# State space mixer of two transformer blocks: another layout of the Toeplitz rows, a later load of the residual, filler products on TensorE, and another order of the last products

## The reference, cut to what matters

```python
lam_bar = jnp.exp(lam * dt)
b_bar = ((lam_bar - 1.0) / lam)[..., None] * b
bu = jnp.einsum('blgc,gpc->blgp', uf.astype(jnp.complex64), b_bar)
_, states = lax.associative_scan(_ssm_binop, (a_elems, bu), axis=1)
y = jnp.real(jnp.einsum('blgp,gcp->blgc', states, c))
y = y + d_skip.astype(f32).reshape(N_GROUPS, SSM_GROUP) * uf
z = jax.nn.gelu(y.reshape(bsz, length, D_MODEL)).astype(u.dtype)
zw = z @ w_glu
val, gate = zw[..., :D_MODEL], zw[..., D_MODEL:]
return val * jax.nn.sigmoid(gate)
```

## Time and profile before

| what | us |
|---|---|
| median of 3 runs | 2467.12 |
| lowest and highest | 2464.04, 2469.94 |
| the profiled execution's own time | 2473.14 |
| its span in the profile | 2471.4 |
| of it, up to the first product of the linear unit | 173.45 |

### The profile page before, as it was taken

One profiled execution on the slowest core, in us unless ns is written; L12 is line 12 of the kernel. 1 busy time (PEld: TensorE's weight loads), 2 busy tenths in 40 slices (PEclk: granted clock), 3 DMA queues, 4 the chain that ended last, 5 costly groups with the idle time before them and its releaser, 6 DMA issues.

```text
span 2471.4 us, 30025 instructions
## 1 busy us (share of the span) xinstructions
PE 2340.3 (95%) x10838; PEld 1938.3 (78%) x10838; DVE 1405.0 (57%) x1986; ACT 880.9 (36%) x1316; POOL 203.2 (8%) x154
## 2 busy tenths in 40 slices
PE   2779999999899999999999999999999899999999
PEld 2677788888788877888877778878888688888887
DVE  6855554456666665454447657773445547654443
ACT  3213332223445533222245435553434443322221
POOL 5502200002100030000020000002000001200000
PEclk7959999999999999999999989999999999999999
DMA  2352232222211112222222211213223212232222
GB/s 114 50 131 84 94 102 94 95 100 94 71 55 58 61 60 94 95 101 94 97 82 78 85 60 54 67 61 109 94 102 128 68 60 94 96 101 94 98 98 85
DMA packets 77174, 213.72 MB, mean 86 GB/s; under 512 B 18320, under 2 KB 26768, under 8 KB 76688
## 3 DMA queue, kind: packets, MB, share of 16 engines
q1 hardware_dynamic: 70880, 205.14, 25.6%
q10 hardware_dynamic: 6192, 7.19, 0.9%
HBM read 203.78 MB, written 4.19 MB: 84 GB/s over the span
## 4 chain that ended last, share of the span: by engine, by line
PE 83%; DVE 6%; ACT 4%; POOL 2%; DMA 2%; issue 2%; SPq 1%; ACTq 0%; DVEq 0%; POOLq 0%
PE lin L423 25%; PE lin L424 25%; PE lin L425 25%; ACT w_hi L811 1%; DVE w_lo L1179 1%; SPq L337 1%; PE tr L690 1%; POOL ssm_cl L1772 1%; PE tr L584 1%; POOL tmp_c L1771 1%; POOL ssm_cl L1770 1%; DMA cols<-cols 1%; DMA ssm_mt<-ssm_kp 1%; DVE fox_pl L1471 1%; PE tr L736 0%
## 5 line engine op out<-in xcount | busy, mean ns | idle before, releaser
L811 ACT ACTIVATE w_hi<-w_raw 128x1024 fp32r<-128x1024 f32 x369 | 390.8, 1059 | 1067.2 <-PE lin L425 1063.7
L423 PE MATMUL lin<-x_hi,w_hi 128*128 128x512 f32 x1472 | 594.8, 404 | 4.4 <-DVE w_lo L1179 2.6
L424 PE MATMUL lin<-x_lo,w_hi 128*128 128x512 f32 x1472 | 575.7, 391 | 0.0
L425 PE MATMUL lin<-x_hi,w_lo 128*128 128x512 f32 x1472 | 575.7, 391 | 0.0
L1179 DVE TENSOR_TENSOR w_lo<-w_raw,w_hi 128x1024 fp32r<-128x1024 f32 x369 | 468.7, 1270 | 110.3 <-ACT w_hi L811 109.6
L423 PEld LDWEIGHTS lin<-x_hi,w_hi 128*128 128x128 f32 x1472 | 278.5, 189 | 72.2 <-issue 9.5
L424 PEld LDWEIGHTS lin<-x_lo,w_hi 128*128 128x128 f32 x1472 | 278.4, 189 | 65.5 <-issue 9.5
L425 PEld LDWEIGHTS lin<-x_hi,w_lo 128*128 128x128 f32 x1472 | 277.8, 189 | 58.8
L423 PE MATMUL lin<-q_hi,w_hi 128*128 128x512 f32 x688 | 271.5, 395 | 7.9 <-DVE q_lo L1184 6.0
L424 PE MATMUL lin<-q_lo,w_hi 128*128 128x512 f32 x688 | 270.7, 394 | 0.0
L425 PE MATMUL lin<-q_hi,w_lo 128*128 128x512 f32 x688 | 270.4, 393 | 0.0
(11 more groups left out here) (405 smaller groups left out, 2858.3 us busy)
## 6 DMA issues: line engine op xcount, KB each, us to landing
w_raw<-w SPq DMA_DIRECT2D x369, 512.0 KB, 3.3
ssm_mt<-ssm_kp SPq DMA_DIRECT2D x64, 64.0 KB, 2.8
ssm_u<-x_a SPq DMA_DIRECT2D x1, 2048.0 KB, 12.2
resid<-x_b ACTq DMA_DIRECT2D x1, 2048.0 KB, 10.6
z_b<-z_scratch SPq DMA_DIRECT2D x4, 512.0 KB, 4.6
out<-resid SPq DMA_DIRECT2D x8, 256.0 KB, 2.1
z_scratch<-ssm_y SPq DMA_DIRECT2D x16, 64.0 KB, 2.3
z_scratch<-ssm_y ACTq DMA_DIRECT2D x16, 64.0 KB, 2.6
```

What stands on the lines that cost most here:

```text
L423: nc.tensor.matmul(out, WH[:, b, w], xh[:, k, 0:cols], start=(k == 0), stop=False)
L424: nc.tensor.matmul(out, WH[:, b, w], xl[:, k, 0:cols], start=False, stop=False)
L425: last = nc.tensor.matmul(out, WL[:, b, w], xh[:, k, 0:cols], start=False, stop=(k == KC - 1))
L811: nc.scalar.activation(WH[:, b, :], raw[:, r, :], ACT.Copy).then_inc(s_hi, 1)
```

## The change

There are four parts.

1. **Layout.** `KP` and `MT` hold the group as the innermost index instead of the second. A Toeplitz DMA then reads and writes one run of 4 KB per partition instead of 8 runs of 512 bytes. In return TensorE reads a within matrix with a step of 8 elements (32 bytes) between columns, ScalarE's copy into `KP` reads PSUM with a step of 128 elements and writes runs of 4, and GpSimd's addition has a step of 8.
2. **Residual.** ScalarE waits for all Toeplitz DMAs before it issues the load of `R`.
3. **Fillers.** `keep_clock(bank, n)` runs n float32 products of the identity with 512 columns of `U` into a bank that nobody needs then: 4 before kernels 2, 5 once VectorE has the block states (a new semaphore `s_mid`), 1 before within 7, and 6 in the first slab of the linear unit.
4. **Order.** within 6 stands between outflow 1 and outflow 2, within 7 between outflow 4 and outflow 5.

```diff
-    MT = at("ssm_mt", 40 * KB, [2, GB, P])
-    KP = ss("ssm_kp", 2 * GB * (2 * CH - 1) * GC * 4, [2, GB, 2 * CH - 1, GC])
+    MT = at("ssm_mt", 40 * KB, [2, CH, GC, GB])
+    KP = ss("ssm_kp", 2 * GB * (2 * CH - 1) * GC * 4, [2, 2 * CH - 1, GC, GB])
...
-            eng.dma_start(MT[j * GC:(j + 1) * GC, b % 2, :, :],
-                          KP[0:GC, b % 2, :, j:j + CH, :].rearrange("p g j c -> p g (j c)")).then_inc(s_mt[b % 2], 16)
+            eng.dma_start(MT[j * GC:(j + 1) * GC, b % 2, :, :, :], KP[0:GC, b % 2, j:j + CH, :, :]).then_inc(s_mt[b % 2], 16)
...
                 for k in range(KC):
                     if ready is not None:
                         pe.wait_ge(s_x, ready(k))
-                    if k == 3 and mid is not None:
+                    if k == mid_at and mid is not None:
                         mid()
...
-                    last = nc.tensor.matmul(WB[b][:, g * NK:(g + 1) * NK], MT[:, b % 2, g, :], U[:, b * GB + g, :],
+                    last = nc.tensor.matmul(WB[b][:, g * NK:(g + 1) * NK], MT[:, b % 2, :, :, g].rearrange("p j c -> p (j c)"), U[:, b * GB + g, :],
...
+            def keep_clock(bank, n):
+
+                for _ in range(n):
+                    nc.tensor.matmul(bank[:], ident[:], U[:, 0:GB, :].rearrange("p g k -> p (g k)"), start=True, stop=True)
...
+            pe.wait_ge(s_vr, BATCHES)
+            keep_clock(WB[5], 4)
+            for b in range(BATCHES - 2):
+                kernels(b + 2)
+                within(b)
+            pe.wait_ge(s_kp, 2 * BATCHES)
+            pe.wait_ge(s_mid, 1)
+            keep_clock(WB[7], 5)
+            for b in range(2):
+                outflow(b)
+            within(6)
+            for b in range(2, 5):
+                outflow(b)
+            keep_clock(WB[7], 1)
+            within(7)
+            for b in range(5, BATCHES):
+                outflow(b)
+
+            def glu_wait():
+
+                pe.wait_ge(s_z, 2)
+                keep_clock(LIN[1], 6)
+            stage("glu", QH, QL, ready=chunks(), mid=glu_wait, mid_at=6)
...
-                    nc.scalar.activation(KP[0:GC, b % 2, 4 * j:4 * j + 4, CH - 1:, :].rearrange("p g j c -> p g (j c)"),
-                                         SC[j][0:GC, :].rearrange("p (g n) -> p g n", g=4), ACT.Copy).then_inc(s_kp, 1)
+                    nc.scalar.activation(KP[0:GC, b % 2, CH - 1:, :, 4 * j:4 * j + 4],
+                                         SC[j][0:GC, :].rearrange("p (g j c) -> p j c g", g=4, j=CH), ACT.Copy).then_inc(s_kp, 1)
...
             act.wait_ge(s_kd, BATCHES)
+            for i in range(2):
+                act.wait_ge(s_mt[i], 16 * CH * BATCHES // 2)
             act.dma_start(R[:], a["x_b"]).then_inc(s_in[1], 16)
...
+            dve.sem_inc(s_mid, 1)
```

More of the change, by code:

```diff
@@ L321, in two_blocks @@
         s_pow, s_xt, s_kd = (sem(n) for n in ("powers_ready", "power_tables", "kp_d_added"))
-        s_state, s_y2, s_z = (sem(n) for n in ("states_ready", "y2_done", "z_ready"))
+        s_mid, s_state, s_y2, s_z = (sem(n) for n in ("block_states_ready", "states_ready", "y2_done", "z_ready"))
         s_zd, s_zb = ([sem(f"{n}{i}") for i in range(ZP)] for n in ("z_dram", "zb_full"))
@@ L408, in _, with linear @@
             c = Counts()
-            def linear(sl, xh, xl, cols=L, mid=None, ready=None):
+            def linear(sl, xh, xl, cols=L, mid=None, ready=None, mid_at=3):
                 b = (sl.at) % 2
@@ L438, in chunks, with stage @@
                 return lambda k: x0 + per * (k + 1)
-            def stage(name, xh, xl, cols=L, ready=None, norm=False):
+            def stage(name, xh, xl, cols=L, ready=None, norm=False, mid=None, mid_at=3):
                 first = ready is not None
                 for sl in slabs(pe, c, name, {}, peel=int(first)):
-                    linear(sl, xh, xl, cols, ready=ready if first else None)
+                    linear(sl, xh, xl, cols, mid if first else None, ready if first else None, mid_at)
                     if first and norm:
@@ L494, in within @@
                 pe.wait_ge(s_mt[b % 2], 16 * CH * (b // 2 + 1))
-                if b == BATCHES - 2:
-                    pe.wait_ge(s_kp, 2 * BATCHES)
                 for g in range(GB):
-                    last = nc.tensor.matmul(WB[b][:, g * NK:(g + 1) * NK], MT[:, b % 2, g, :], U[:, b * GB + g, :],
+                    last = nc.tensor.matmul(WB[b][:, g * NK:(g + 1) * NK], MT[:, b % 2, :, :, g].rearrange("p j c -> p (j c)"), U[:, b * GB + g, :],
                                             start=(g == 0), stop=False)
@@ L501, in _, with outflow @@
             pe.wait_ge(s_b0, 2)
[L502 to L512, removed]
+            def keep_clock(bank, n):
+                for _ in range(n):
+                    nc.tensor.matmul(bank[:], ident[:], U[:, 0:GB, :].rearrange("p g k -> p (g k)"), start=True, stop=True)
+            def outflow(b):
+                for part in range(1, len(PARTS)):
+                    if b * GB == PARTS[part - 1]:
+                        pe.wait_ge(s_state, part)
                 for g in range(GB):
@@ L517, in _ @@
                 last.then_inc(s_y2, 1)
-            stage("glu", QH, QL, ready=chunks())
+            kernels(0)
+            kernels(1)
+            pe.wait_ge(s_vr, BATCHES)
[19 more added lines that the diff above has]
+            stage("glu", QH, QL, ready=chunks(), mid=glu_wait, mid_at=6)
             def mlp(name):
@@ L1778, in _ @@
                 pool.wait_ge(s_kp, 2 * (b + 1))
-                lag0 = KP[0:GC, b % 2, :, CH - 1, :]
+                lag0 = KP[0:GC, b % 2, CH - 1, :, :].rearrange("p c g -> p g c")
                 g_.tensor_tensor(lag0, lag0, DK[0:GC, b * GB:(b + 1) * GB, :], ALU.add).then_inc(s_kd, 1)
```

## The result

| | us |
|---|---|
| median of before, 10 runs beside those of after | 2468.2 (2464.04 to 2471.27) |
| median of after, 10 runs | 2477.13 (2473.17 to 2479.63) |
| ratio, 95% interval | 1.0035 [1.0025, 1.0045] |
| the profiled execution of after, its span | 2477.12, 2475.4 |

The change made the kernel slower by 8.9 us (2477.13 - 2468.2), where 2467.0, no change, was forecast. The range ended at 2475.

The account below looks back on a forecast made before the run. It took the chain through VectorE's scan, the outflow batches, mostly at half clock, and a fixed 21.2 us road to chunk 6 as the bound. Outputs -6.2, six fillers +5.5 and step +0.4 gave -0.3 on 2467.12: 2467.0, range 2460 to 2475.

Parts of the forecast that it names:

- Access with a step: Stepped reads in the within batches: up to 1.9 times the time, once on the path (within 7), 0 to +1.7, taken +0.4 us.
- rival (b): Stepped weight reads make TensorE the bound before the outflow batches, from about 4 us per within batch; +17 to +34 us, chance 0.10.
- the forecast's 135.3: Time in us when VectorE's scan has the first part of the states, before which outflow 0 cannot start.
- Toeplitz issue at 0.33: SyncE's issue of a Toeplitz DMA falls from 603 ns to 0.33 us, as for a one-run weight load; worth nothing by itself.
- The late residual: Load of R behind the Toeplitz DMAs, near 122 us: the 11.16 us landing goes, at no cost.
- The outputs, -3.2 to -11.2, chosen -6.2: Sixth outflow batch bound by the scan ends earlier than 166.33: -3.2 us all at half clock, -11.2 all at full.
- two of the five batches at full clock: Choice for outflow 2 to 5 and within 7: two escape half clock, -3.0 us on top of -3.2.
- rival (a): The clock holds through all outputs: -11.2 + 5.5 = -5.7 us, 2461.4; chance 0.17.
- The 4 early fillers: Before kernels 2: fill the 5.57 us pause with 3.7 us of work and keep the clock up for the within products.
- The road of 21.2 us: From the end of the sixth outflow batch through DRAM to the start of chunk 6 in the linear unit: 21.2 us, unchanged.
- The six fillers, +5.5: In the linear unit, behind the wait for chunk 6, they delay the chain by their full length: +5.5 us, bounds 0 and 11.
- the full-clock price: Cost of the linear unit's fillers at full clock: 0.92 us a product, 5.5 us for six, against 11 at half clock.

## Why the prediction was wrong, point by point

**The step that failed** is "Access with a step", of which the prediction said: "It stands once on the path (within 7), so 0 to +1.7. I take a quarter, +0.4", with "At half clock a batch is 3.5 anyway, and it may be hidden there". A stepped within batch measured 4.0 us at either clock, against 2.0 at full and 3.5 at half clock contiguous. The factor 2 at full clock was inside the bounds. The wrong part was how often it stands on the path. With 7.0 us a pair TensorE needs 97.39 to 136.6 for six within and five kernels batches and is the bound all that way, so the price is paid six times, and the slack to the scan is gone; the prediction had these batches done by 117 to 125. A second part was in no term of the sum: the clock fell in every within batch but the first, which ran at half clock already, and made the kernels batches 3.0 us in place of 1.92. With kernels batches of 1.92 and within batches of 4.0 the same eleven would take 6 x 4.0 + 5 x 1.92 = 33.6 us and end near 131, an estimate from these rows, ahead of the scan at 136.2. What makes the clock fall there, without a pause, no run shows. TensorE as the bound is rival (b), which had 0.10. Its deciding point, "about 4 us per within batch", was right, and the kernel landed just past it. Its price was too high (17 to 34 us), because it assumed twice the time at half clock as well, and the measurement shows 4.0 and not 7.3.

The five fillers turned the near miss into a loss (0.36 us lay between the scan's first part, ready at 136.24, and the end of within 5). They wait for VectorE's block states, which had been ready since 129, and nothing skips them when TensorE is late. They were costed at nothing with the pause before outflow 0 as cover; the cover was gone. By the trace, 1.3 us behind the forecast's 135.3 and 5.4 of fillers put outflow 0 at 142.0. In medians the layout costs 6.7 us, and the forecast had +0.4 for its step and nothing for a lower clock. The forecast missed 2477.13 by 10.1 us.

The Trainium skill's rule in "SBUF — State Buffer", section "Door 1: The DMA port swizzle", was weighed and given too small a chance. The trace agrees that a read which leaves a 16-byte line at each element pays in full (0.238 to 0.25 us a pass with step 8). That section gives two marks for where this starts, and they differ: at least two accesses to a line for full bandwidth, and a free stride of up to 4 float32 elements. The measurement bears out the first, since step 2 costs 0.118 at full clock, and not the second, since step 4 costs 0.234. So the measurement decides: two float32 elements.

**Toeplitz issue at 0.33: wrong, without effect.** 0.59 was measured. The pattern was compared with a load from DRAM into 128 partitions; the number of runs is not what sets the price, since it is 591 ns with one run and 603 with eight.

**The late residual, without a term of its own in the sum.** The long landing did go, as the prediction said (3.2 us at most in after, 11.2 before). Alone, in the kernel before, it brings 3.7 us in the median (ratio 0.9985). There the outputs stand behind within 6 and 7, which wait for the DMAs. With the new order outflow 0 doesn't wait for them, and order and residual together bring the same 3.5 us (ratio 0.9986). The load was forecast to be issued near 122 us and went out at 144.55 in after and 136.30 with the old layout. The road to chunk 6 (20.9 us) shows no harm from it.

**The outputs, -3.2 to -11.2, chosen -6.2: too good by some 2 us.** With the old layout the sixth outflow batch ended at 162.4, 4.0 before 166.35. Right was the mechanism: the scan binds (134.95, 143.90), there is a pause (3.4 us, and 2.4 in the version without the six), the clock falls about there (144.6 and 144.2), and the single filler before within 7 raises it only sometimes: not in after nor in these two, but in the version with twelve fillers. There, as in the version with three fillers behind within 6, the clock had fallen at 137 and no such pause was left (0.16 us with twelve). Wrong were the "two of the five batches at full clock": hardly one. Three fillers at its place give four to five of them, and a kernel 11.4 us faster than before in the median (0.9954), which is the upper end of the term, and about rival (a) without the six fillers (-11.2).

**The 4 early fillers, meant to "keep the clock for the within products": wrong.** The clock fell at 97.6 in after, as it did at 96.8 in the kernel before. A pause of 2.99 us was still left ahead of within 0 (5.57 before).

**The road of 21.2 us: right**, 20.9.

**The six fillers, +5.5: right as a length, with a small rest.** From start to start they hold the engine for 5.55 us in the version with three fillers in the outputs, 1.3 us of it at half clock, and for 6.7 us in after, 3.8 of it at half clock. In the median the former is 6.7 us. The pairs with and without them in the changed and the old layout gave 8.4 us and 0.0037 (9.1 us), with some 3 us of uncertainty each. That they stand behind the wait was read rightly from the order, but before the wait they cost as much, since the pause there is only 0.5 us. The argument for the full-clock price, that the cold stretch is there in both, holds in the traces: the fillers take over the half-clock stretch in which chunks 6 and 7 ran before. From chunk 6's inputs to the second slab it takes 20.4 us in after (189.44 to 209.81) and 15.6 in before (187.52 to 203.14), 4.8 us more.

**The sum** by the runs: order and late residual -3.5, the ten fillers ahead of the linear unit -3.7 (0.9986 to 0.9971; the intervals overlap, and the trace shows no such gain, so this is not shown), the six +9.1, the layout +6.7: +8.6. The four terms are the steps of one way from before to after, so that they add up to the measured ratio (1.0035, 8.6 us) is no proof of any of them. The forecast's terms were -6.2, +5.5 and +0.4.

What stays open: why six fillers cost 1 to 3 us more in medians than their length, and more still than the 4 to 5 us that the traces show at the second slab; why the order brought 2.4 us in the trace and nothing in the median; and why the clock fell in the stepped within batches.

## What to carry to other kernels

When a change makes each instruction of an engine dearer, add up the engine's whole stretch against the next event that it has to meet, not just the one instance on today's path; here six within batches, each 0.5 to 2.0 us dearer, and the lower clock of the batches between them used up a slack that one batch would not have touched. And read the granted clock by batches, not by the mean of a stretch: 0.72 hid that one kind of batch ran at full clock and the other at half. Keep TensorE's float32 weights contiguous or at most two elements apart; the short runs of the DMA that the layout removed had cost nothing on the path. Filler products paid here only ahead of 64-column products that else ran at half clock; ahead of 512-column products, which raised the clock by themselves within 5 us, or where TensorE is the bound, they cost nearly their own length.

## What the runs showed of the hardware

- A weight read with a step of 4 or 8 float32 elements costs 0.23 to 0.25 us a pass at either level of the clock, and one of step 16 0.217 at half clock. At half clock, where a contiguous pass takes 0.213, a step is therefore nearly free, and at full clock (0.110) it doubles the pass. Step 2 costs 0.118 and 0.213.
- TensorE's clock fell from its upper to its lower level without a pause. In after TensorE was busy for 30.61 of the 31 us from 97 to 128, and from 104 to 139 the clock fell five times, each time in a stepped within batch, and rose again behind it.
- ScalarE's read from PSUM with a step of 128 elements, written in runs of 16 bytes, costs no more than the contiguous one. This is its copy in after, two at once, and the same row in the version with the old layout:

```profile
132.64 1.06 ACT L909 ACTIVATE ssm_kp<-sc 16x512 f32<-16x512 f32 x2 [5.80 <-PE sc L488]
```

```profile
124.67 1.06 ACT L910 ACTIVATE ssm_kp<-sc 16x512 f32<-16x512 f32 x2 [3.40 <-DMA ssm_mt<-ssm_kp]
```

- Three 512-column fillers, 4.1 us of them on the chain, saved 8 us of the products behind them by raising the clock from its lower level (1.2 GHz) to the upper (2.4 GHz). One such filler, 10 us later, was followed by no rise in after and in five other profiled versions, and by a rise 1.3 us behind it in the one with twelve fillers in the linear unit.
